# A decoder layer with routed experts on Trainium2: the front in two halves of tokens, 192 dot products ahead, four gathered tiles in place of three

## The reference, cut to what matters

```python
hn = rmsnorm(h, g_mix); proj = hn @ w_in
# group a: 8 heads of 64, causal, distances in three dilated windows
# group m: 8 heads of 96 (64 + 32 rotary), dense causal, values of 64
h = h + concat(o_a, o_m) @ w_out
t = rmsnorm(h, g_ffn)
q = (t @ w_pq).reshape(-1, 8, 2, 128)
sc = einsum('thpc,hpnc->thpn', q, sub_keys)      # 128 keys on each side
vals, idx = top_k(sc, 16)                        # then the best 16 of 16 x 16 sums
expert = i1 * 128 + i2; gate = softmax(best)
act = gelu(einsum('td,thkd->thk', t, u_emb[expert]))
h = h + einsum('thk,thkd->td', act * gate, v_emb[expert])
out = rmsnorm(h, g_final)
```

## Time and profile before

| what | us |
|---|---|
| median of three runs | 3618.78 |
| lowest, highest run | 3610.1, 3626.18 |
| the profiled execution: its time | 3583.56 |
| the profiled execution: its span | 3581.8 |
| TensorE, weight load, VectorE, ScalarE, GpSimd busy | 3234.6, 2533.0, 2257.9, 1030.3, 976.2 |

### The profile page before, as it was taken

One profiled execution on the slowest core, in us unless ns is written; L12 is line 12 of the kernel. 1 busy time (PEld: TensorE's weight loads), 2 busy tenths in 40 slices (PEclk: granted clock), 3 DMA queues, 4 the chain that ended last, 5 costly groups with the idle time before them and its releaser, 6 DMA issues.

```text
span 3581.8 us, 48342 instructions
## 1 busy us (share of the span) xinstructions
PE 3234.6 (90%) x17405; PEld 2533.0 (71%) x17405; DVE 2257.9 (63%) x5536; ACT 1030.3 (29%) x1403; POOL 976.2 (27%) x941
## 2 busy tenths in 40 slices
PE   8996998889799983666999999999999999999997
PEld 4444666664587773665988878878878888788885
DVE  2112334543289988995888877777777777644544
ACT  2212333431233324883222222222112222222222
POOL 0000000000012221001333335656556656332222
PEclk9996878999899997998999999999999999999999
DMA  4113111110211110669777879999999999766665
GB/s 184 50 50 114 23 25 34 37 29 36 101 65 61 47 44 1 188 180 316 259 258 258 272 250 365 376 371 354 366 358 382 362 369 378 272 242 246 249 226 192
DMA packets 331453, 715.63 MB, mean 200 GB/s; under 512 B 72960, under 2 KB 166400, under 8 KB 329856
## 3 DMA queue, kind: packets, MB, share of 16 engines
q0 software_dynamic: 110592, 402.70, 30.7%
q1 hardware_dynamic: 213648, 299.95, 24.2%
q10 hardware_dynamic: 7024, 10.51, 0.8%
HBM read 637.58 MB, written 75.50 MB: 199 GB/s over the span
## 4 chain that ended last, share of the span: by engine, by line
PE 49%; DVE 2%; DMA 1%; issue 1%; ACT 0%; POOL 0%; another core or an unknown queue 0%; POOLq 0%; ACTq 0%; DVEq 0%
PE psum L1720 23%; PE psum L1704 21%; PE psum L1747 5%; DMA w<-scr_g 1%; DVE res L1894 1%; DVE res L1883 1%; DVE u_lo L1851 0%; DMA rows<-scr_rows 0%; DVE w_lo L1868 0%; DMA v_ring<-v_rows,eidT 0%; POOL v_ring L1688 0%; DVE v_lo L1873 0%; ACT u_hi L1782 0%; DVE w L1863 0%
## 5 line engine op out<-in xcount | busy, mean ns | idle before, releaser
L1688 POOL DMA_INDIRECT v_ring<-v_rows,eidT x384 | 441.8, 1151 | 617.4 <-PE psum L1747 508.6
L1704 PE MATMUL psum<-hn_hi_e,u_hi 128*128 128x320 f32 x1792 | 556.6, 311 | 27.4 <-DVE w L1863 19.4
L1704 PE MATMUL psum<-hn_lo_e,u_hi 128*128 128x320 f32 x1792 | 555.8, 310 | 0.6 <-issue 0.6
L1704 PE MATMUL psum<-hn_hi_e,u_lo 128*128 128x320 f32 x1792 | 555.2, 310 | 0.7 <-issue 0.7
L1720 PE MATMUL psum<-v_hi,w_hi 128*128 128x512 f32 x1280 | 511.6, 400 | 21.3 <-DVE res L1883 10.6
L1883 DVE TENSOR_TENSOR res<-psum,res 128x512 f32<-128x512 f32 x640 | 431.8, 687 | 125.0 <-PE psum L1720 112.7
L1720 PE MATMUL psum<-v_hi,w_lo 128*128 128x512 f32 x1280 | 501.0, 391 | 0.0
L1720 PE MATMUL psum<-v_lo,w_hi 128*128 128x512 f32 x1280 | 500.9, 391 | 0.0
L1681 POOL DMA_INDIRECT res<-u_rows,eid x288 | 337.5, 1172 | 339.9 <-DVE dots L1894 279.9
L1894 DVE CUSTOM_DVE_ANT_0 res<-res,rows 128x1024 f32<-128x1024 f32 x288 | 349.8, 1220 | 53.8 <-DMA res<-u_rows,eid 31.1
L1704 PEld LDWEIGHTS psum<-hn_hi_e,u_hi 128*128 128x128 f32 x1792 | 338.3, 189 | 32.3 <-issue 28.0
(11 more groups left out here) (246 smaller groups left out, 5020.0 us busy)
## 6 DMA issues: line engine op xcount, KB each, us to landing
v_raw<-v_rows SPq DMA_DIRECT2D x128, 512.0 KB
u_raw<-uT SPq DMA_DIRECT2D x112, 512.0 KB
w<-scr_g SPq DMA_DIRECT2D x128, 320.0 KB
scr_g<-gates SPq DMA_DIRECT2D x4, 8192.0 KB, 30.5
scr_m<-st_m SPq DMA_DIRECT2D x8, 1024.0 KB
w_raw<-in_w_pq SPq DMA_DIRECT2D x8, 1024.0 KB, 7.1
u_raw_r<-uT SPq DMA_DIRECT2D x16, 512.0 KB, 3.5
scr_g<-gates SPq DMA_DIRECT2D x1, 7680.0 KB, 30.9
```

Of the source, the lines that this page charges most:

```text
L1688: pool.indirect_dma_start(v_ring[:, m % V_RING, :], None, core.i["v_rows"], bass.IndirectOffsetOnAxis(eidT[:, m // P, t:t + 1], 0)).then_i ...
L1704: last = nc.tensor.matmul(ps[:, a, 0:COLS], x[:, c, j, :], y[:, j, a * COLS:(a + 1) * COLS], start=m == 0, stop=m == len(terms) - 1)
```

## The change

The layer is reordered. After project_in the first four tiles go through attend (both groups), project_out and route; then the other four do. SPT becomes 4, so the first half is exactly the sparse tiles and the second exactly the dense ones. route gets `sparse`: the sparse half makes only expert numbers, their transpose and gates, the dense half only slots and the early columns, of which there are now 8 of 512 tokens (PRE = 8, one in 16). `attend` gets the range `i0` to `i1` of query tiles; keys below `i1` are all loaded and turned, so a head has 2 fills in the first half and 3 in the second. `w_out`, the masks and `w_pq` are loaded twice, and the weight splits are made twice.

In the second half's attention the dots run ahead: GpSimd gathers the first 192 rows of `u` (96 for each group of heads), and VectorE takes three dot products after the output of each of the 64 units. `shared` is True for both groups, so ScalarE and VectorE go on taking turns with the copies.

In run_experts the dense part has 4 tiles: 24 products of 512 an activation, in two alternating PSUM banks, and 8 fills a group. The remaining 320 dots are spread over groups 0 to 53, and the 128 quads over groups 1 to 63, 96 of them up to group 54 and 32 in the last nine. `rows` has two buffers.

```diff
-SPT = 3
+SPT = 4
-PRE = 16
-PRE_STEP, PRE_AT = 8, 3
+U_RING, V_RING = 4, 8
+PRE = 8
+PRE_STEP, PRE_AT = 16, 3
+HT = NT // 2
+AHEAD = 192
...
-def attend(core, mix, mask, group, heads, dim, scr, q_at, k_at, v_at, mix_at):
+def attend(core, mix, mask, group, heads, dim, scr, q_at, k_at, v_at, mix_at, i0, i1, ahead=None):
...
+    M = i1 - i0
+    shared = ahead is None or ahead.shared
+    N = M * 2
...
-            head_fills[k] = [fill(("qk", k, z, half)) for z in range(2) for half in range(2)]
+            head_fills[k] = [fill(("qk", k, z, half)) for z in range(2) for half in range((i0 // 4, 0)[z], i1 // 4)]
...
+        if ahead is not None:
+            @block.gpsimd
+            def _(pool):
+                for n in range(ahead.start, ahead.stop):
+                    if n >= core.U_RING:
+                        pool.wait_ge(ahead.dot_ready, n - core.U_RING + 1)
+                    pool.indirect_dma_start(res[:, n % core.U_RING, :], None, core.i["u_rows"],
+                                            bass.IndirectOffsetOnAxis(ahead.eid[:, n // P, n % P:n % P + 1], 0)
+                                            ).then_inc(ahead.u_row_in[n % core.U_RING], 16)
...
+            def beside(it, x):
+                if ahead is not None:
+                    done, units = it * N + x, heads // 2 * N
+                    share = ahead.stop - ahead.start
+                    for n in range(done * share // units, (done + 1) * share // units):
+                        dot(ahead.start + n)
...
                         nc.vector.tensor_scalar(mix[:, i - i0, bass.ds(it * (2 * ev) + (mix_at + k * ev), ev)],
                                                 ps[:, 6 + b, 0:ev], rden[:, x:x + 1], None, ALU.mult).then_inc(o_out, 1)
+                        beside(it, x)
...
-                for a in range(ACTS):
-                    for m, (x, y, j) in enumerate(terms):
-                        last = nc.tensor.matmul(ps[:, a, 0:COLS], x[:, c, j, :], y[:, j, a * COLS:(a + 1) * COLS],
+                for m, (x, y, j) in enumerate(terms):
+                    last = nc.tensor.matmul(ps[:, r % 2, :], x[:, c, j, :], y[:, j, :],
...
+    NQ = NS // QUADS
+    DOTS_END, TURN_LAST = 54, 54
+    REST = NS - AHEAD
+    HEAD_Q = NQ - QUAD
+    dot_at = [AHEAD + min(REST, REST * g // DOTS_END) for g in range(NG + 1)]
+    quad_at = [HEAD_Q * max(g - 1, 0) // TURN_LAST if g <= TURN_LAST + 1 else
+               HEAD_Q + QUAD * (g - TURN_LAST - 1) // (NG - TURN_LAST - 1) for g in range(NG + 1)]
...
+            for g in range(NG):
+                us = dots_of(g)
+                vs = range(quad_at[g] * QUADS, quad_at[g + 1] * QUADS)
+                steps = max(len(us), len(vs))
+                for k in range(steps):
+                    for m in range(k * len(vs) // steps, (k + 1) * len(vs) // steps):
+                        v_row(vs[m])
+                    for n in range(k * len(us) // steps, (k + 1) * len(us) // steps):
+                        u_row(us[n])
...
+            first, hn_hi, hn_lo = front(0, None)
+            route(core, hn_hi, hn_lo, True, None, eid, eidT, sgate)
+            first.close()
...
+                parts = [Ahead(z * AHEAD // 2, (z + 1) * AHEAD // 2, eid, rows, dots, rows_in, u_row_in, dot_ready, True)
+                         for z in range(2)]
+                second, hn_hi, hn_lo = front(HT, parts)
...
+            route(core, hn_hi, hn_lo, False, slotT, eid, eidT, sgate)
```

More of the change, by code:

```diff
@@ L2 @@
 from contextlib import ExitStack
+from dataclasses import dataclass
 import concourse.bass as bass
@@ L107, in _ @@
                 sp.sem_clear(s)
+@dataclass
+class Ahead:
+    start: int
+    stop: int
+    eid: object
+    rows: object
+    dots: object
+    rows_in: object
+    u_row_in: list
+    dot_ready: object
+    shared: bool
 class Core:
@@ L702, in _, with dot, rounds, heads_pair @@
             own = Own(dve, core.dve_own)
-            with dve.Fori(0, heads // 2) as it:
+            def dot(n):
+                if n == ahead.start:
+                    dve.wait_ge(ahead.rows_in, 16)
+                dve.wait_ge(ahead.u_row_in[n % core.U_RING], 16 * (n // core.U_RING + 1))
+                x = res[:, n % core.U_RING, :]
+                nc.vector.tensor_tensor_reduce(out=x, in0=x, in1=ahead.rows[:, n // P, :], scale=1.0, scalar=0.0,
+                                               op0=ALU.mult, op1=ALU.add,
+                                               accum_out=ahead.dots[:, n // P, n % P:n % P + 1]
+                                               ).then_inc(ahead.dot_ready, 1)
+            def beside(it, x):
[4 more added lines that the diff above has]
+                        dot(ahead.start + n)
+            def rounds(body):
+                if ahead is not None:
+                    for it in range(heads // 2):
+                        body(it)
+                else:
+                    with dve.Fori(0, heads // 2) as it:
+                        body(it)
+            def heads_pair(it):
                 for kind, x in order:
@@ L1076, in _ @@
+                        pe.wait_ge(sc_out, ONE + (it * 4 + b * 2 + z - 1 if b or z else it * 4))
+                        for i in range(HT):
+                            last = nc.tensor.matmul(ps[:, 4 + z, i * P:(i + 1) * P],
                                                     qT[:, z, i * P:(i + 1) * P], keysT[:, z, :], start=True, stop=True)
                         last.then_inc(sc_done, 1)
-                    early(it * 4 + b * 2 + 1)
+                    if not sparse:
+                        early(it * 2 + b)
@@ L1080, in _ @@
             pe.wait_ge(slot_ready, 1)
-            for i in range(SPT):
-                last = nc.tensor.transpose(ps[:, 2, i * P:(i + 1) * P], eid_f[:, i, :], core.ident[:, :])
-            last.then_inc(eidT_done, 1)
-            for i in range(NDT):
+            if sparse:
+                for i in range(SPT):
+                    last = nc.tensor.transpose(ps[:, 2, i * P:(i + 1) * P], eid_f[:, i, :], core.ident[:, :])
+                last.then_inc(eidT_done, 1)
+            for i in range(0 if sparse else NDT):
@@ L1552, in reals @@
             return sum(place(m) is None for m in range(n))
+        real_ids = [n for n in range(NKEY) if place(n) is None]
         def before(n):
@@ L1751, in sums @@
                 last.then_inc(sums_done, 1)
-            nexts = [0]
-            def catch_up(step):
-                while nexts[0] < NS // QUADS and sum_step(nexts[0] * QUADS + QUADS - 1) <= step:
-                    sums(nexts[0])
-                    nexts[0] += 1
             pe.wait_ge(hn_in, 32)
@@ L1764, in _ @@
                 activations(g + 1, 0)
-                catch_up(g * STEPS - 1)
+                quads = quads_of(g)
+                for q in quads[:len(quads) // 2]:
+                    sums(q)
                 for tile in turns(g):
```

518 lines of the change are left out of this document (274 added, 244 removed).

## The result

The changed kernel takes 3723.44 us, median of four runs (3716.91 to 3739.1), against 3615.47 for the kernel before, run beside it: a ratio of 1.0308, 95% interval 1.0259 to 1.0356. It is slower, by 108 us where 39 were forecast. The profiled execution took 3739.1 us, the slowest of its four; the one of before, 3583.56, is among that kernel's fastest.

What follows compares the result with a forecast made beforehand. TensorE was taken to bound the experts' stage and output projection, VectorE route and spread, no engine attention. Terms -232 + 242 + 22 + 46 - 47 + 8 = +39 us, giving 3658 us on the median; range 3545 to 3765.

Steps and rivals of the forecast that it cites:

- The gathers hide: Second-half attention: three rows each 6 us, 0.26 TB/s, stay below what the trace moves, so gathers cost nothing.
- some 10 us that the dots don't fill: Second-half attention, per pair of heads: time for two head starts and refilling the pipeline at the pair's end.
- the dots don't hide at all: Second-half attention, rival: each row lands late on a ring of four; placed inside the low-clock case, no chance of its own.
- The dots themselves: Second-half attention with dots on VectorE: a pair of heads takes 63 us in group a, 56 in m, 476 in all.
- The low-clock rival: Attention: pauses from VectorE's dots drop TensorE's clock in both groups, 70 us a second-half pair, whole 3772; chance 0.12.
- Its other part: First-half attention in the low-clock case: 236 us in all, +30.
- The transfers rival: Experts' stage: transfers bound it at 366 GB/s, costing 50 us instead of 20, whole 3688; chance 0.13.
- The stage came 18 us over: Experts' stage: forecast to change by -232 us, with TensorE's work going from 1859 to 1617.
- some 76 us: Experts' stage: what it held beyond TensorE's work before, mostly its start, the change of `rows` and the end.
- The first half, project_out, route and spread: First-half attention units 206 us; project_out twice +22; route twice +46, its TensorE pauses covered by VectorE; spread -47.

Runs made afterwards that it cites:

- wide_act_256: The changed kernel with dots one by one, all second-attention copies on ScalarE, 128-row scores in both groups, and 256 early dots in place of 192: 3639.19 us.
- dots_alone: The changed kernel with the 192 early dots kept but their gathers and VectorE's wait for the row taken out: 3656.34 us.
- wide_act: The changed kernel with dots one by one, all second-attention copies on ScalarE, and 128-row scores in both groups: 3555.87 us.
- ahead128: The changed kernel with dots one by one and 128 early dots in place of 192: 3670.55 us.
- one_by_one: The changed kernel with one dot behind each mask, each turn's copies and each output, in place of three behind each output: 3652.05 us.

## Why the prediction was wrong in size

**The step that failed** is "The gathers hide: three rows each 6 us are 0.26 TB/s, below what the trace moves; a row slot is freed about 6 us before its next use." The term priced at 0 cost 76 us of trace time (582 against 506). Evenness was what failed in the changed kernel: the rows nearly hide when dots are spread (6.4 us of waits, at 2.6 us a row) and don't when nine come together (54.0, at 3.0 us a row). The rate was no safe argument either: three rows each 6 us is the pace of wide_act_256, where VectorE waited 102.4 us though its dots were spread. That 0.26 TB/s lie below what the transfers move elsewhere did not tell what a ring of four hides. The prediction had noted, one paragraph up, copies behind dots at the head starts and the refill at the pair's end, as "some 10 us that the dots don't fill"; it took that as lost time and not as the place where the dots pile up. The rival "the dots don't hide at all", which named VectorE waiting for `res<-u_rows`, was set aside by the same 6 us.

**The dots themselves** were priced well: without gathers 506 us from first mask to last output, against 4 x 63 + 11 + 4 x 56 = 487. So of the 95 us by which the changed kernel exceeded 487, the late rows are 76 and the dots themselves 19. The reason given did not hold, though. In group a the working took half a pair at each clock; the runs show nearly the low one throughout (0.58 and 0.55), and TensorE as the bound until dots fill VectorE. In group m it took the full clock; the clock fell from 1.00 to 0.74 as soon as dots stood there. The pairs of dots_alone, 67.3 and 57.5 us, lie near the 63 and 56 partly by luck.

**The low-clock rival** (70 us a pair) came close in numbers: 68.4 and 76.7. Its other part, 30 us more in the first attention, did not come (pairs of 29.6 and 22.3 us there). Its mechanism, pauses that bring the clock down, fits group m. The Trainium skill, "TensorE: Matmul & The Clock Gate", section "A second HAM failure mode: psum-queue depth-cycling", has that; these runs agree for group m (1.00 to 0.74). For group a it is no explanation: there the clock was 0.50 without a pause, and 0.99 with pauses once the products had 128 rows.

**The transfers rival** is answered by three windows of the experts' stage, with 128, 192 and 256 early dots: at 192 early dots the stage is TensorE's. Over 400 us of it the changed kernel moved 380 GB/s while TensorE idled under 5 us:

```profile
2200.00:2600.00 400.00, 395.48 (x1928) 287.32 (x1927) 305.30 (x447) 93.99 (x122) 248.86 (x209) 1.00 0.98 380
```

So the 366 of the earlier trace rows was no limit. Nor was the 358 that the Trainium skill gives in "DMA: Bandwidth & Descriptors", section "Specifications", as a core's limit, a stack's 716 halved for two cores; on this kernel's one core the trace disagrees, at 380. The stage came 18 us over: TensorE's work 24 over, 1641 against 1617, and its idle time 6 under, 92 against 98 (the "some 76 us" of the prediction should have been 1947 - 1859 = 88; only its changes entered the sum). Of the 92 us, 42 are waits for `v_ring`, 35 of these from 3460 us on, about where the last nine groups and their 32 quads stand. Whether a smoother end would save these was not tried.

**The first half, project_out, route and spread** were right within 13 us each. In route the granted clock is 0.75 and 0.86 where it was 0.93; as forecast, VectorE's time covered it.

**The whole.** In the changed kernel 192 dots cost 582 - 400 = 182 us of the second attention, 0.95 each; spread out they cost 100, 0.52 each, and beyond 192 it is 1.2 (on wide_act). What one buys in the experts' stage is 1.1 us between 128 and 192 and next to nothing beyond. The last 64 are therefore worth having where they are spread, at 0.6 us each (ahead128), and not worth much as they were placed. What the first 128 buy was not run: the run without dots leaves them out altogether. The stage's gain of 1947 - 1733 = 214 us does not pay for 237 + 619 - 514 = 342 us of attention.

## What to carry to other kernels

Price work put into another engine's pauses by its densest bunch and by the pace at which the ring that feeds it turns, not by its mean rate against what the transfers move, and look where the loop has its seam. Before moving work, ask what each piece buys at the margin: the bound of the stage that is relieved can change on the way. When a stage of matrix products stands at half clock with no pause, look at how many rows they contract over before anything else.

## What the runs showed of the hardware

Scores over 64 rows of contraction kept TensorE at a granted clock of 0.50 (1.2 GHz) through stretches without idle time. The same products over 128 rows, half of them zeros, ran at 0.99 (2.4 GHz), with no change in columns or instructions. In the kernel before that is worth 81 us by medians, 69 by the ratio, for 64 more partitions of two tiles and two clears of memory. With 96 rows (group m) the clock was full already where no dots stood (1.00), and going to 128 changed nothing (3597 against 3595 us). Products over 64 rows with early dots beside them stood at 0.52 to 0.60 in the windows read, those over 128 at 0.72 to 0.78. Why the rows of contraction matter no run shows.

A gather of one 4 KB row for each of 128 tokens landed 5.2 to 5.7 us after its issue (medians of one_by_one, the changed kernel and wide_act_256 in the second attention), and the ring of four gave VectorE a row each 2.02 us, averaged over a pair of heads, and no run went faster (wide_act_256, at 271 and 277 GB/s).
